# The product of a unit with its values, in one piece ahead of the last C scores instead of two halves around them

## The reference

```python
def gqa_attend(q, k, v):
    s = jnp.einsum('bqhgd,bshd->bhgqs', q, k).astype(jnp.float32) * (q.shape[-1] ** -0.5)
    p = jax.nn.softmax(s, axis=-1).astype(v.dtype)
    return jnp.einsum('bhgqs,bshd->bqhgd', p, v)

def diff_attend(q, k, v, lam):
    ...
    a = (jax.nn.softmax(s1, axis=-1) - lam * jax.nn.softmax(s2, axis=-1)).astype(v.dtype)
    return jnp.einsum('bhqs,bshd->bqhd', a, v)
```

## Time and profile before

| | us |
|---|---|
| median of 3 runs | 3407.63 |
| lowest and highest | 3406.36, 3410.68 |
| the profiled execution, first to last instruction (span) | 3405.5 |
| PE, DVE, ACT, POOL busy | 3196.2, 2153.8, 1324.6, 1131.3 |
| full blocks of the attention, layer 0 | about 412 to 789 |
| full blocks of the attention, layer 1 | about 2181 to 2557 |

### The profile page before, as it was taken

The page is one execution under the profiler, slowest core; times in us unless marked ns, Lnnn a source line. Parts: engine busy times, 40 slices in busy tenths (PEclk is TensorE's granted clock), DMA queues, the critical chain, the costliest instruction groups (busy, mean ns, idle before and its releaser), DMA issues. The chain is left out here.

```text
span 3405.5 us, 49521 instructions
## 1 busy us (share of the span) xinstructions
PE 3196.2 (94%) x18000; PEld 2566.4 (75%) x18000; DVE 2153.8 (63%) x3314; ACT 1324.6 (39%) x2061; POOL 1131.3 (33%) x1155
## 2 busy tenths in 40 slices
PE   6989899999999999999998899899999699999997
PEld 4876577777788888888886786677777578888885
DVE  4754587876644444444447764578875667777677
ACT  3431466664421122111112441466664333333332
POOL 1333455552110000000002332355551465555653
PEclk9999999999999999999999999999999899999998
DMA  6557300104321111111105466201013111111113
GB/s 241 194 181 282 140 23 33 35 20 164 110 64 37 37 37 37 37 37 37 37 31 190 151 224 249 101 33 35 32 62 138 65 53 55 51 47 53 55 52 118
DMA packets 189957, 304.92 MB, mean 90 GB/s; under 512 B 13446, under 2 KB 139918, under 8 KB 178534
## 3 DMA queue, kind: packets, MB, share of 16 engines
q1 hardware_dynamic: 187685, 302.04, 25.7%
q10 hardware_dynamic: 2113, 0.77, 0.1%
HBM read 234.58 MB, written 68.19 MB: 89 GB/s over the span
## 5 line engine op out<-in xcount | busy, mean ns | idle before, releaser
L132 PE MATMUL banks<-h_hT,up_u_hi 128*128 128x512 f32 (+1 forms) x1056 | 375.3, 355 | 7.1 <-DVE up_u_lo L2031 5.7
L133 PE MATMUL banks<-h_hT,up_u_lo 128*128 128x512 f32 (+1 forms) x1056 | 374.8, 355 | 0.0
L134 PE MATMUL banks<-h_hT,up_u_hi 128*128 128x512 f32 (+1 forms) x1056 | 374.6, 355 | 0.0
L132 PE MATMUL banks<-ff_d_lo,ff_a_hi 128*128 128x512 f32 x792 | 317.9, 401 | 22.3 <-DVE ff_acc L2614 9.6
L134 PE MATMUL banks<-ff_d_hi,ff_a_hi 128*128 128x512 f32 x792 | 310.7, 392 | 0.0
L133 PE MATMUL banks<-ff_d_hi,ff_a_lo 128*128 128x512 f32 x792 | 310.4, 392 | 0.0
L2463 POOL TENSOR_TENSOR ff_ms<-ff_ss,c_eps 128x1 f32<-128x1 f32 x10 | 11.2, 1116 | 894.5 <-ACT ff_t_gate L2574 894.5
L2614 DVE TENSOR_TENSOR ff_acc<-banks,ff_acc 128x512 f32<-128x512 f32 x220 | 150.7, 688 | 175.3 <-PE banks L134 175.1
L1586 PE MATMUL banks<-c_ident,al_prA 128*128 128x128 f32 x1312 | 214.4, 277 | 20.0 <-ACT al_oTC L1889 18.6
L3198 DVE TENSOR_TENSOR h_acc<-banks,h_acc 128x512 f32<-128x512 f32 x336 | 225.1, 689 | 4.1 <-PE banks L134 0.9
L132 PEld LDWEIGHTS banks<-h_hT,up_u_hi 128*128 128x128 f32 x1056 | 200.3, 190 | 36.0 <-issue 5.9
(11 more groups left out here) (372 smaller groups left out, 8127.3 us busy)
## 6 DMA issues: line engine op xcount, KB each, us to landing
kv_m_wm<-in_w_mod_dram SPq DMA_DIRECT2D x40, 1024.0 KB, 5.2
up_u_raw<-in_w_up_dram SPq DMA_DIRECT2D x44, 512.0 KB, 3.8
ff_d_raw<-in_w_down_dram SPq DMA_DIRECT2D x44, 512.0 KB, 3.3
hT_d<-fr_hs SPq DMA_DIRECT2D x20, 1024.0 KB, 5.3
st_hs<-hT_d SPq DMA_DIRECT2D x20, 1024.0 KB, 7.1
q_d<-fr_qs SPq DMA_DIRECT2D x18, 512.0 KB, 2.8
q_d<-fr_qs SPq DMA_DIRECT2D x36, 256.0 KB, 3.0
al_quA<-q_d SPq DMA_DIRECT2D x18, 512.0 KB, 3.9
```

The costliest lines, as they stand in the source:

```text
L132: e.matmul(out, w[0], x[1], start=start, stop=False)
L133: e.matmul(out, w[1], x[0], start=False, stop=False)
L134: return e.matmul(out, w[0], x[0], start=False, stop=stop)
```

## The change

`values_a` and `values_c` lose their second argument. Each does the whole product where its first half stood, that is ahead of `rest_c`; nothing of it is left behind `rest_c`. `out_a` in a C step stands behind the whole C product. The list `turns`, and so the ring's places, stay as they are, and so do the lists of the other engines.

```diff
-            def values_a(u, part):
-                if part == 0:
-                    e.wait_ge(outA_act, actA[4 * u + 3])
-                    e.wait_ge(outA_dve, dveA[4 * u + 3])
-                    emptied(e, "PVA", u, 0)
+            def values_a(u):
+                e.wait_ge(outA_act, actA[4 * u + 3])
+                e.wait_ge(outA_dve, dveA[4 * u + 3])
+                emptied(e, "PVA", u, 0)
                 pv, n_keys = bank("PVA", u, 0), keys_of(4 * u)
-                for k in range(part * n_keys // 2, (part + 1) * n_keys // 2):
+                for k in range(n_keys):
...
-                if part == 1:
-                    ins.then_inc(pvA_done, 1)
+                ins.then_inc(pvA_done, 1)
...
                 if unit_at(n, PV_A) is not None:
-                    values_a(unit_at(n, PV_A), 0)
+                    values_a(unit_at(n, PV_A))
                 if unit_at(n, PV_C) is not None:
-                    values_c(unit_at(n, PV_C), 0)
+                    values_c(unit_at(n, PV_C))
                 if unit_at(n, O_A) is not None:
                     out_a(unit_at(n, O_A))
                 if whole:
                     rest_c(n)
-                if unit_at(n, PV_A) is not None:
-                    values_a(unit_at(n, PV_A), 1)
-                if unit_at(n, PV_C) is not None:
-                    values_c(unit_at(n, PV_C), 1)
```

More of the change, by code:

```diff
@@ L1606, in values_a, with values_c @@
                                        start=(k == 0), stop=(k == n_keys - 1))
-                if part == 1:
-                    ins.then_inc(pvA_done, 1)
[L1610 to L1614, removed]
+                ins.then_inc(pvA_done, 1)
+            def values_c(u):
+                e.wait_ge(outC_act, actC[2 * u + 1])
+                e.wait_ge(outC_dve, dveC[2 * u + 1])
+                emptied(e, "PVC", u, 0)
                 pv, n_keys = bank("PVC", u, 0), keys_of(4 * u)
-                for k in range(part * n_keys // 2, (part + 1) * n_keys // 2):
+                for k in range(n_keys):
                     for half in range(2):
@@ L1619, in values_c @@
                                        start=(k == 0), stop=(k == n_keys - 1))
-                if part == 1:
-                    ins.then_inc(pvC_done, 1)
+                ins.then_inc(pvC_done, 1)
             def out_a(u):
```

## The result

The changed kernel takes 3506.47 us (median of 4 runs, 3502.48 to 3507.17) against 3408.93 for the kernel before (3406.36 to 3410.68): ratio 1.0283, 95% interval 1.0269 to 1.0297, 97.5 us slower. Forecast were 3476 and 3463 to 3490. The sign and the place were right, but the time lies 16 us above the range and 30 us above the forecast.

What follows compares the result with a forecast made beforehand. PE was taken as nearly full, held by the ring's bank in C steps; 26.7 + 15.6 + 16.4 + 9.6 = 68.3 us on the median 3407.6 gave 3476 us, range 3463 to 3490.

Steps and rivals of the forecast that it cites:

- What bounds the stage: Attention's full blocks: PE nearly full, busy 44.65 of 46.31 us per two units, already waiting for the bank in C steps.
- the chain: Full blocks: a later `rest_c` delays the copy freeing the bank PE needs for transposes; A steps have 0.59 us spare.
- Terms (2) to (5): Losses per step: plain A 1.57, A with norm 1.20, plain C 1.09, C with squares 0.64 us; 68.3 us in all.
- The C terms: C steps: 1.09 us lost in each of 15 plain ones, 0.64 in each of 15 with squares.
- The A terms: A steps: 1.57 us lost in each of 17 plain ones, 1.20 in each of 13 with the norm.
- PE's clock falls: Rival, chance 0.06: stops in full blocks bring half-clock stretches, up to 1.7 us per unit, 51 us in all, 3527 us.
- the likeliest: Case with chance 0.82: the bank holds PE for both products in the full blocks; own range 3465 to 3488 us.
- The seam's gain: Product in one piece saves PE 0.15 to 0.25 us per product step, but in front of a wait.
- DVE as the next to be late: Plain A steps: DVE's `max_a` for the next step would cost 0.4 us without the bank's hold, but is covered.
- Signs (a) to (d): Full blocks: longer bank holds, two-unit period 50.8 us, A-step `rest_c` 4.47 us after product start, plain `rest_c` released by PE.
- (a): PE idle before its transposes for the A copy, about 1.5 us plus the saving; C hold above 0.58 us.
- (e): PE's granted clock stays at 1.00 through the full blocks.

Runs made afterwards that it cites:

- the split: Kernel before, with six or eight of the A product's ten key tiles ahead of the last C scores instead of five: 3411.5 and 3436.0 us.

## Why the prediction was wrong, point by point

- **What bounds the stage, and the chain** (`rest_c`, `max_c`, `exp_c`, copy, transposes): right, to 0.01 us in each link from `rest_c` to PE's release, and shown by the changed kernel with the copies first and by the split.
- **Terms (2) to (5)**, 68.3 us: right in sum. The period came to 50.9 in place of 46.3; the scoring steps lost 68.9 us without the clock, 69.4 with the stops filled. The C terms were right alone (48.0). The A terms alone were 0.6 us per two units too small, for the squares' wait on GpSimd; with the A product alone whole PE waits 6.5 us for `max_a` ahead of `rest_c` from 430 to 780, in 7 waits of up to 0.9, and in the changed kernel, where the longer C product stands ahead of `rest_c`, not at all.
- **The step that failed** is in the rivals: "*PE's clock falls*" at 0.06, as a case that excludes the likeliest. It was not an alternative but came on top, and the sum had no term for it: 27.3 us of a miss of 30; the other 3 are in the other phases. Its price per stretch, up to 1.7 us, was 1.5; there were 18 stretches for 60 events. What misled was "the context's steps [...] had 27.16 of 31.6 = 86% and kept a granted clock of 1.00". The same busy share does not tell: the kernel with the A product alone whole ran at 315.78 of 350 = 90% without one stretch in the full blocks, that with the C product alone whole at 322.04 of 350 = 92% with two, and the changed kernel had windows of 25.44 us at 22.28 = 88% and 1.00.
- **The range** took in that case only as 0.06 of chance. With the clock as a term on top, up to its own 51 us, it would have reached from 3465 to 3527.
- **The seam's gain**: right that the time does not show it. The trace does: in the A step the transposes start 679.95 - 675.26 = 4.69 us behind the product's start instead of 4.94, in front of the wait.
- **DVE as the next to be late**: its pass over the A scores does not hold `rest_c` in the changed kernel, as worked out; not seen was that its small operations stretch with GpSimd's place, which bears on every experiment on the order of ACT.
- Signs (a) to (d) came, (a) smaller than said (1.33 us), (e) did not. The clock was named there as what would make the prediction wrong.

## What to carry to other kernels

Splitting a long PE block around a small matmul that feeds another engine isn't about the small matmul: ask what stands behind it in the lists of all engines until PE itself waits, and how much of the delay is spare; here 0.59 us of 2.16. A stop put on a nearly full PE can cost twice, once as the wait and once as a lower clock, and about 1.3 us of useless work in each stop told the two apart here. The cheaper repair was on the other end: the copy that frees the bank goes ahead of the long exponential. It pays where the product is finished by then: in the kernel before, the C copy in front gave 15.5 us and both copies in front nothing.

## What the runs showed of the hardware

- VectorE's operation with two SBUF inputs (128x256, `al_sq`) takes 0.42 us when GpSimd runs nothing beside it. When GpSimd's long addition (L1822 in the kernel before) is running as it starts, it ends 0.28 to 0.35 us behind GpSimd, in all the traces: 1.00, 1.42, 1.56, 2.04, 2.94 us in these kernels. The Trainium skill ("SBUF — State Buffer", "SBUF: two separate sides") calls the shared port pair "an exclusive lock, not a bandwidth split"; the trace agrees, for the case that GpSimd starts first. A shift of GpSimd by 0.43 us was one of VectorE by 0.42.
- PE's granted clock fell to 0.50 for 3.4 us at a time, 18 times, in full blocks in which PE's longest single stop was 1.34 us and PE was busy 88%, and did not fall with about 1.3 us of matmuls or of transposes put into each stop. Why one kernel at 90% has no such stretch and another at 92% has two is left open.
